# One kernel, 288 tokens, 32 experts: the block counts taken ahead of the gates, and a semaphore of their own for the weight loads

## The reference

```python
logits = jnp.einsum('td,de->te', x2, w_router) + b_router
top_vals, top_idx = lax.top_k(logits, TOP_K)          # 4 of 32
gates = jax.nn.softmax(top_vals, axis=-1)
...
def expert_block(args):
    xb, e = args
    gu = xb @ w_up[e] + b_up[e]                        # w_up[e]: 1024 x 2048
    gate, up = gu[:, :D_EXPERT], gu[:, D_EXPERT:]
    gate = jnp.minimum(gate, SWIGLU_LIMIT)
    up = jnp.clip(up, -SWIGLU_LIMIT, SWIGLU_LIMIT)
    act = (up + 1.0) * (gate * jax.nn.sigmoid(SWIGLU_ALPHA * gate))
    return act @ w_down[e] + b_down[e]                 # w_down[e]: 1024 x 1024
...
y = jax.ops.segment_sum(out * row_gate[:, None], row_tok, num_segments=n_tok)
```

## Time and profile before

| | |
|---|---|
| runs | 1377.78, 1378.38, 1382.91 us; median 1378.38 us |
| profiled execution | 1379.41 us, its span 1377.6 us |
| busy share of the span | PE 87%, DVE 37%, ACT 19%, POOL 5% |
| mean granted clock of TensorE | 0.950 of full speed |
| DMA | 448.91 MB, 326 GB/s over the span |

### The profile page before, as it was taken

How to read it: one execution, slowest core, us unless ns; L and a number is a source line. 1 busy time by engine, 2 the same in 40 slices (tenths; PEclk the granted TensorE clock), 3 DMA queues, 4 the chain that set the end, 5 groups by cost and what they waited for, 6 DMA issues and landing times.

```text
span 1377.6 us, 28967 instructions
## 1 busy us (share of the span) xinstructions
PE 1193.3 (87%) x11107; PEld 582.5 (42%) x11108; DVE 516.4 (37%) x1236; ACT 255.4 (19%) x497; POOL 67.6 (5%) x69
## 2 busy tenths in 40 slices
PE   5889999999889997887689669868799798689996
PEld 3667777775434342333233224313234243234333
DVE  0789961221433333323133223313233233133334
ACT  3001122200212221211112112212122122122222
POOL 0293210000000000000000000000000000000000
PEclk9999999999799999999899999999899899899999
DMA  9962333331497799999999999999999999999992
GB/s 260 317 203 93 130 117 113 111 128 59 152 402 320 299 393 416 419 417 418 418 405 394 417 418 396 420 418 418 417 414 395 417 396 420 418 418 395 393 393 88
DMA packets 110946, 448.91 MB, mean 326 GB/s; under 512 B 8526, under 2 KB 42894, under 8 KB 78107
## 3 DMA queue, kind: packets, MB, share of 16 engines
q1 hardware_dynamic: 110190, 446.57, 81.8%
q10 hardware_dynamic: 685, 1.17, 0.3%
q0 software_dynamic: 48, 0.85, 0.2%
HBM read 447.00 MB, written 2.42 MB: 326 GB/s over the span
## 4 chain that ended last, share of the span: by engine, by line
PE 62%; DMA 22%; DVE 7%; SPq 3%; POOL 3%; issue 3%; ACT 0%; POOLq 0%; DVEq 0%
PE banks L1229 22%; DMA ring<-in_w_up 22%; PE banks L1036 12%; PE banks L1239 10%; PE banks L1018 4%; PE banks L969 4%; DVE R L710 4%; PE banks L997 3%; SPq L373 3%; PE banks L1148 2%; POOL big L433 2%; PE banks L1004 2%; PE banks L1027 2%; DVE big L695 1%; POOL prod L455 1%
## 5 line engine op out<-in xcount | busy, mean ns | idle before, releaser
L1229 PE MATMUL banks<-ring,big 128*32 128x512 f32 x3328 | 448.8, 630 | 126.0 <-DMA ring<-in_w_up 113.2
L304 DVE TENSOR_TENSOR xt<-xt,banks 128x1024 f32<-128x1024 f32 x106 | 129.1, 1219 | 499.5 <-PE banks L1018 499.5
L1239 PE MATMUL banks<-ring,R 128*32 128x256 f32 x3328 | 223.8, 388 | 1.2 <-DVE R L919 1.2
L1229 PEld LDWEIGHTS banks<-ring,big 128*32 128x32 f32 x3328 | 95.2, 112 | 279.1 <-DMA ring<-in_w_up 172.4
L1036 PE MATMUL banks<-hT,ring 128*128 128x288 f32 x768 | 195.6, 417 | 7.9 <-ACT stage L483 5.9
L1239 PEld LDWEIGHTS banks<-ring,R 128*32 128x32 f32 x3328 | 113.5, 113 | 168.0 <-issue 134.8
L1036 PEld LDWEIGHTS banks<-hT,ring 128*128 128x128 f32 x768 | 149.6, 196 | 50.1 <-ACT stage L483 6.3
L602 ACT COPY R<-banks 128x256 f32<-128x256 f32 x52 | 19.3, 372 | 517.8 <-PE banks L1239 517.8
L710 DVE SCALAR_TENSOR_TENSOR R<-big,convw,R 128x256 f32<-128x256 f32 x240 | 99.3, 494 | 0.0
L906 DVE TENSOR_TENSOR big<-banks,bupT 128x512 f32<-128x512 f32 x52 | 36.0, 692 | 138.2 <-PE banks L969 138.2
L1018 PE MATMUL banks<-R 32*128 32x256 f32 x848 | 77.0, 434 | 0.7 <-ACT R L602 0.7
(11 more groups left out here) (217 smaller groups left out, 680.3 us busy)
## 6 DMA issues: line engine op xcount, KB each, us to landing
ring<-in_w_up SPq DMA_DIRECT2D x256, 1024.0 KB, 11.1
ring<-in_w_down SPq DMA_DIRECT2D x128, 1024.0 KB, 9.6
ring<-in_w_in SPq DMA_DIRECT2D x24, 1024.0 KB, 10.1
ring<-in_w_branch_b SPq DMA_DIRECT2D x4, 1024.0 KB, 5.0
ring<-in_w_branch_a SPq DMA_DIRECT2D x4, 1024.0 KB, 4.9
ring<-in_w_out SPq DMA_DIRECT2D x4, 1024.0 KB, 5.0
xt<-in_x_prompt SPq DMA_DIRECT2D x2, 512.0 KB, 3.9
out_y_prompt<-xt SPq DMA_DIRECT2D x2, 512.0 KB, 2.7
```

The lines of the kernel that those rows point to most:

```text
L304: nc.vector.tensor_tensor(dst, dst, rows, ALU.add).then_inc(y_added, 1)
L1229: ins = mm(UP[g * BLK:(g + 1) * BLK, :], xT[:, k, :], ring[:, k, g * 512:(g + 1) * 512], start=k == 0, stop=k == UP_SLOTS - 1)
L1239: ins = mm(DN[q * BLK:(q + 1) * BLK, 0:256], actT[:, f % 4, f // 4, :], ring[:, UP_SLOTS + j, h * D + q * 256:h * D + (q + 1) * 256], star ...
```

## The change

On VectorE the block counts (compares, reduce, prefix sum, `items_before`, `n_bodies`) stand ahead of `take_x(0)`. The eight compares are one operation with the round limits taken from `slot_ids`. `items_before` has a semaphore of its own, `before_known`, and SyncE's wait ahead of its loop is for this one. After `take_x(0)` come the list, the gates, the copy of the list, and then the weights `comb`. On TensorE the list's transpose stands after up(3), the gates' product after up(5), and the bias product after up(7).

```diff
+        before_known = sem("before_known")
...
-            sp.wait_ge(items_known, 1)
+            sp.wait_ge(before_known, 1)
             with sp.Fori(1, NE) as e:
                 before = sp.value_load(items_before[0:1, bass.ds(e - 1, 1)], min_val=0, max_val=MAX_ITEMS)
...
-            take_x(0)
-            dve.wait_ge(exped, 1)
-            link(V.tensor_tensor(gates[:], gates[:], mask[:], ALU.mult))
...
-            ins.then_inc(comb_ready, 1)
-
             dve.wait_ge(counted, 1)
-            for r in range(1, MAX_ROUNDS):
-                ins = V.tensor_scalar(need[:, r - 1, :], DN[:, 0:NE], float(BLK * r), None, ALU.is_gt)
-            link(ins)
+            link(V.tensor_tensor(need, DN[:, 0:NE].unsqueeze(1).to_broadcast([P, MAX_ROUNDS - 1, NE]),
+                                 slot_ids[:, BLK:MAX_ROUNDS * BLK:BLK].unsqueeze(2).to_broadcast([P, MAX_ROUNDS - 1, NE]),
+                                 ALU.is_gt))
...
+            V.tensor_scalar(items_before[:], src[0:1, :], 1.0, None, ALU.subtract).then_inc(before_known, 1)
+            V.tensor_scalar(n_bodies[:], src[0:1, NE - 1:NE], 1.0, None, ALU.subtract)
+            take_x(0)
...
             V.tensor_tensor(item_column, item_column, item_expert, ALU.mult).then_inc(listed, 1)
-            V.tensor_scalar(items_before[:], src[0:1, :], 1.0, None, ALU.subtract)
-            V.tensor_scalar(n_bodies[:], src[0:1, NE - 1:NE], 1.0, None, ALU.subtract)
+
+            dve.wait_ge(exped, 1)
+            link(V.tensor_tensor(gates[:], gates[:], mask[:], ALU.mult))
...
             dve.wait_ge(list_turned, 1)
             V.tensor_copy(items[:], DN[0:1, 0:P]).then_inc(items_known, 1)
+            dve.wait_ge(gates_kept, 1)
+            for tt in range(NT):
+                ins = V.tensor_scalar(comb[:, tt], slot_ids[:, 0:BLK].unsqueeze(1).to_broadcast([P, QN, BLK]),
+                                      rankm[:, tt, 0:1], gates[:, tt, 0:1], ALU.is_equal, ALU.mult)
+            ins.then_inc(comb_ready, 1)
...
                 up(k, 16 * (FILLS + 1))
-                if k == 4:
+                if k == 3:
+                    pe.wait_ge(listed, 1)
+                    tr(DN[0:1, 0:P], item_column).then_inc(list_turned, 1)
+                if k == 5:
                     pe.wait_ge(gates_kept, 1)
...
-                if k == 6:
-                    pe.wait_ge(bdown_in, 16 * QN)
-                    pe.wait_ge(combT_ready, 1)
-                    combine(0, row_out[0])
-            pe.wait_ge(listed, 1)
-            tr(DN[0:1, 0:P], item_column).then_inc(list_turned, 1)
+            pe.wait_ge(bdown_in, 16 * QN)
+            pe.wait_ge(combT_ready, 1)
+            combine(0, row_out[0])
```

More of the change, by code:

```diff
@@ L889, in _ @@
             V.tensor_tensor(item_column, item_column, item_expert, ALU.mult).then_inc(listed, 1)
-            V.tensor_scalar(items_before[:], src[0:1, :], 1.0, None, ALU.subtract)
-            V.tensor_scalar(n_bodies[:], src[0:1, NE - 1:NE], 1.0, None, ALU.subtract)
+            dve.wait_ge(exped, 1)
+            link(V.tensor_tensor(gates[:], gates[:], mask[:], ALU.mult))
+            link(V.tensor_reduce(ss[:, 12:12 + NT], gates[:], AX.X, ALU.add))
+            link(V.reciprocal(ss[:, 12:12 + NT], ss[:, 12:12 + NT]))
+            V.tensor_tensor(gates[:], gates[:], ss[:, 12:12 + NT].unsqueeze(2).to_broadcast([P, NT, NE]), ALU.mult
+                            ).then_inc(gates_kept, 1)
             dve.wait_ge(list_turned, 1)
             V.tensor_copy(items[:], DN[0:1, 0:P]).then_inc(items_known, 1)
+            dve.wait_ge(gates_kept, 1)
[3 more added lines that the diff above has]
+            ins.then_inc(comb_ready, 1)
             dve.wait_ge(items_known, 1)
```

## The result

Six runs of the changed kernel gave 1368.6 to 1373.29 us, median 1372.11; the kernel before, now with six runs, has a median of 1379.15. The ratio is 0.9935, 95% interval 0.9913 to 0.9957: by the ratio about 9 us faster, by the two medians 7.0. The changed kernel ran again with two later sets of runs, beside the kernel before on the same chip: 1370.61 against 1379.78 (ratio 0.9928, 0.9914 to 0.9943) and 1371.43 against 1380.02 (0.9929, 0.9911 to 0.9947); the medians differ by 9.2 and 8.6 us there. The profiled execution took 1368.6 us, its span is 1366.9.

A forecast was written before the change was run, and what follows sets the result against it. Expert 1's w_up loads, waiting for an unneeded list, were taken to bound body 1. Issuing them 10.15 us earlier, with TensorE's limit moving too, gave 10.1 us gain: 1369.3 from the profile, 1368.3 from the median, so 1368.8; range 1366.5 to 1372.5.

The forecast's parts named there:

- What bounds the kernel: Ahead of body 1: expert 1's w_up loads wait for a list they don't need, then 19.42 us of DMA.
- Part 1, the counts: VectorE's counts first: merged compare 0.45 us, before_known at 362.45 us, 1.0 us of cover ahead of take_x(0).
- the dear compare: VectorE's compare if merging gains nothing: 0.87 us, leaving 0.5 us of cover ahead of take_x(0).
- Part 2, the loads: SyncE waits for counts alone: first w_up load of expert 1 at 366.2, 10.15 us earlier; slot 7 lands at 389.85.
- the lower bound: Expert 1's load stream: slot 0 alone in flight for 1.7 us, lost in full, leaves a gain of 8.5 us.
- Part 3, TensorE: TensorE's reordered first pass still ends near 374.3; gap 0.7 us, gather of body 0 at 375.0.
- both limits: End of the pass on slot 7: 390.85 by TensorE alone, 390.9 by DMA; both move by 10 us.
- Does it last: Body 1 and later: each later load moves by the same 10 us; nothing gained or lost after body 1.
- The sum: Whole kernel: gain 10.1 us, bounds 8.5 and 11.3, giving 1368.8 us.
- TensorE as the new limit: Rival: register work isn't hidden, gather of body 0 stays at 377.27; gain 7.1 us, 1371.8 us; chance 0.15.
- The wait at take_x(0): Rival: counts' chain 3 us longer eats 1.0 us cover and 2 us gain, 1370.9 us; chance 0.08.
- Code loading: Rival: instruction block TensorE needs ahead of body 0 waits 20 us behind the eight loads, 1389 us; chance 0.03.

The follow-up runs named there:

- e2: The changed kernel, but SyncE waits for items_known (the list) again instead of before_known; 1374.93 us, ratio 0.9964 to the kernel before.
- e4: The changed kernel with five extra VectorE sums into an unread scratch tile ahead of take_x(0); 1372.0 us, ratio 0.9946 to the kernel before.
- e5: The changed kernel with the eight separate compares in place of the merged one; 1369.26 us, ratio 0.9930 to the kernel before.
- e1: The changed kernel with list, gates and TensorE's order as before; early counts and SyncE's before_known wait stay; 1375.45 us, ratio 0.9955.
- e6: The changed kernel with the gates' product after up(4) and the bias product after up(6) again; 1370.93 us, ratio 0.9933 to the kernel before.
- e8: The changed kernel, but TensorE reads n_bodies into its register after up(3), behind the list's transpose; 1368.86 us, one run.
- e3: The changed kernel unchanged, profiled and run again; 1370.61 us against 1379.78 for the kernel before, ratio 0.9928.

## Why the prediction came out as it did

**What bounds the kernel.** Right. e2 puts the wait for the list back and the DMA comes back into the chain with the same 23.67 us from first load to landing.

**Part 1, the counts.** Right in each term: the compare 0.42 us (0.45 taken), cover 1.08 us (1.0), and a late take_x(0) costs its lateness once the cover is gone (e4). With the dear compare 0.63 us are left, 0.5 forecast (e5).

**Part 2, the loads.** Right: first load at +2.14 (2.14 forecast), slot 7 landed at 390.46, which is the forecast 389.85 and the 0.6 us by which this execution's up(0) was later. That the stream took the same 23.65 us is in part luck: by the views of the single loads slot 1 landed 3.2 us after slot 0 (before 2.5), which is the slow start that the lower bound stood for, and the one long interval later in the stream was 3.3 us in place of 3.9. The load issued first landed 4.8 us after its issue, in the kernel before and in the changed one alike. The figure of the Trainium skill ("DMA: Bandwidth & Descriptors", "Bandwidth"), 6.15 us for 1 MB by itself, was not borne out by that row; the 78% that I gave with it as a share of a long stream's rate stand there as a share of the peak, and the long stream of that table has 97%. The longer streams of e1 and e5 don't bear it out either: their first loads took 4.9 and 4.8 us.

**Part 3, TensorE.** The size of the gap was right (0.66 us, 0.7 taken) and the reason was not: I put it down to the bias product's wait for ScalarE's copy, and e6 took that wait away and had a larger gap. It is the register work, 2.5 us, less the 1.7 to 1.8 us that the instruction stream is ahead (e8). That the old gap of 3.07 us was TensorE's register work was right, though the row names VectorE's selection (L678): this ended at about 376.5, and TensorE's last register step stood at 377.2. I also had both limits meet at +27.8; the first profile gave +27.96, set by TensorE, with the limit from the landing less than 0.2 us sooner (e8). What was mis-sized is the first pass: I let it end as before, but it took 375.80 - 364.66 = 11.14 us, not 10.34, since the clock left its lower level 1.6 us later after up(0)'s start. With the gap, the pass on slot 7 ended at 392.33 - 364.66 = 27.67, 0.9 us later than the 26.8 forecast for TensorE alone. It cost little, since from there to body 1 it took 0.29 us; the 1.0 that I had added is what the DMA limit needs. The gather of body 0 ran at full clock, as forecast.

**Does it last.** Right as far as the runs can tell: from body 1 to the end the difference to the one profile of the kernel before is within the scatter.

**The sum.** A gain of 10.1 us was forecast, the distance to body 1 shrank by 10.0, the three sets of runs gave ratios of 0.9928 to 0.9935, 9.0 to 9.9 us. The predicted time of 1368.8 is 3.3 under the first median, which lies only 0.4 under the high end of the range, 1372.5; and that end was set for TensorE as the new limit, which did not come. So the mechanism is sized rightly, and that the time stayed in the range is in part luck. The scatter of the mixing half (5 us between profiles) is more than the 0.6 to 0.7 us that three runs of the kernel before had led me to allow.

**The rivals.** "TensorE as the new limit" is what happens without TensorE's part of the change: e1 has it, with 1.90 us for the gather at the lower clock and +30.79 against the 30.84 worked out. The wait at take_x(0) was made in e4 and costs what was said. Code loading shows no stop: from up(0) to body 1 TensorE's chain in the changed kernel has no gaps but 0.66, 0.23 and 0.29 us, and e3 repeats the distances to 0.01 us. Nothing beyond that was tried on it.

## What to carry to other kernels

Ask of each wait what the waiting engine reads, and give that value a semaphore of its own; but look for the next limit beside it before counting the gain, since here the loads alone gave 7.2 of 10 us, and the last 2.8 needed the other engine's order too. Register loads count as work: place them where the engine still has more queued than they last, check every engine that does them, and look at which wait stands just ahead of them in the stream. And after a router's short matmuls look at the granted clock of what follows.

## What the runs showed that I had not expected

TensorE's instruction stream was 1.7 to 1.8 us ahead of its matmuls at the end of the first slot pass, whether slot 7's ups (e6) or the bias product (changed kernel) stood last. So a landing can delay the next body though it comes before the matmuls need the slot (e8).

Six matmuls of 256 columns in the router's waits kept the clock at its upper level in both profiles with them, and made the stretch from turn to up(0) 2.3 to 2.6 us shorter than in the changed kernel and its other variants. In the kernels without them the clock stayed low even where the window rows show TensorE busy all the time (by matmul ends that the profile models), as in these rows of e3 (the second number is its busy time of the 2.00 us, the granted clock the third from the end):

```profile
360.00:362.00 2.00, 2.00 (x9) 1.87 (x9) 0.60 (x3) 0.28 (x1) 0.00 (x0) 0.50 1.04 422
362.00:364.00 2.00, 2.00 (x18) 0.94 (x18) 1.38 (x5) 0.00 (x0) 0.00 (x0) 0.50 1.02 406
```

The Trainium skill ("TensorE: Matmul & The Clock Gate", "HAM oscillation — how this bites in real kernels") ties the fall to waits for DMA between short bursts of matmuls; here, by the waits of the changed kernel from 350 to 370 us, TensorE waited for VectorE and ScalarE and for no DMA.

The time from the start of the kernel to the end of the mixing half differs by up to 5 us between executions of the same code. In the three profiles of the changed kernel it makes up 3.8 of the 4.3 us between the shortest and the longest span. Why it differs was not tried.
